# A hybrid decoder trunk in fp32: the last MLP's down projection, columns 1024 to 2047, by one level of Strassen

## The chip, the cores and the metric

The program runs on one core of a Trainium2 chip, one launch. The metric is the device time of that launch in microseconds, the median of several runs.

## The reference, cut to what matters

Two pre-norm residual layers over 256 tokens with 2048 features, float32. Each layer has a mixer (attention and retention heads in the first; state-space groups and a gated convolution in the second), a cross attention into 256 memory tokens, and an MLP with a hidden width of 8192:

```
def sq_relu_mlp(xn, w1, w2):
    return jnp.square(jax.nn.relu(xn @ w1)) @ w2

for layer in range(2):
    h = h + mixer(rmsnorm(h, norm_mix[layer]))
    h = h + cross_attention(rmsnorm(h, norm_xattn[layer]), memn, ...)
    h = h + sq_relu_mlp(rmsnorm(h, norm_mlp[layer]), mlp_w1[layer], mlp_w2[layer])
return rmsnorm(h, norm_final)
```

w1 is 2048x8192 and w2 is 8192x2048. The change is in the product with w2 of the second (last) MLP.

## The kernel before, in words

**Precision.** Every matmul operand is a sum of a high part (fp32r, one pass of TensorE) and a low part (what rounding left). A product is three matmuls: high by high, high by low weights, low activations by high weights (lines 636 to 638). For each weight half ACT copies the raw fp32 weights into the high part `whi` (line 1267), and DVE subtracts it from the raw ones into `wlo` (line 1838). That pair of steps is called a split here.

**Slabs, halves and the ring.** Weights come in slabs of 1 MB (`raw`, four buffers; the DMAs are issued by SP, lines 408 and 423, when DVE has split what was there). A slab is two halves of 256 rows by 512 columns. `whi` and `wlo` have four places each (RING = 4), used in order: half n goes into place n mod 4. ACT may write place n when PE has used half n-4 (semaphore `half_used`); DVE waits for ACT (`hi_ready`), PE for DVE (`lo_ready`). A unit is eight halves.

**A chunk of the MLP.** The hidden width is cut into 8 chunks of 1024. A chunk is four units: two head units, each making 512 hidden values with the tokens as the moving operand (per half 8 wide matmuls of 512 columns, line 1073, and 8 narrow ones of 256, line 1081; two halves are taken together, first both wide groups, then both narrow ones, and the other way round in the last two halves); then two pair units of the down projection, for output columns 0 to 1023 and 1024 to 2047 (per half 12 matmuls of 512 columns). The first chunk's first unit has another form ("wide").

**PSUM.** `acc` has four banks, two for a block, and blocks alternate between the two pairs. A unit of either kind fills two blocks. PE waits on `acc_free` before it opens one. For a head unit's banks that release comes from DVE's reduction into `hid` (line 2223), for a pair unit's from DVE's adds into `h` (line 1886, two operations of 128x512, one for each 128 tokens). `tp` and `at`, two banks each, are used by transposes and attention, not by the MLP's later chunks.

**The order of the work.** Each engine runs a list written out by hand. On ACT and DVE a unit is a loop over i = 0..7: split half i, then what the slot i holds. On DVE: in the first head unit of a chunk, slots 1 and 2 hold the adds into `h` of the previous pair unit (columns 1024 to 2047); in the second head unit and the first pair unit, slots 0, 1, 2 hold the four reductions of the unit before (0; 1; 2 and 3), slots 3 and 5 the low part of the squared hidden values (line 2231); in the second pair unit slots 1 and 2 hold the adds of columns 0 to 1023. ACT does relu and square of the hidden values in slots 2 and 4 (lines 1624 to 1627), with the high part into `yt`. Chunks 1 to 6 of the last MLP run in a hardware loop, one chunk per trip. The scale of the norm is applied at the adds (`rstd[:, 14]`, the square of the reciprocal root, since the squared relu is homogeneous).

At the end, POOL multiplies `h` by the final gain (vector loaded by a DMA), and ACT and DVE finish the last norm.

Of the kernel before, what the change touches and what calls it, by code (L numbers as in the profile page):

```python
# [23 lines left out]
F32 = mybir.dt.float32  # L24
# [4 lines left out]
ALU = mybir.AluOpType  # L29
AX = mybir.AxisListType  # L30

P = 128
# [71 lines left out]


def trunk(nc, x, mem, norm_final, ab_w_in, ab_b_forget,
          ab_w_out, cd_w_in, s5_d, s5_w_glu, cd_w_out, xa_wq, xa_wkv, xa_wo, mlp_w1, mlp_w2,
          rope, decay_in, tri, causal, eye, x_t, mem_t, gains, s5_rates, s5_bc, fb_d, out):
    ctx = ExitStack()
    with ctx:  # L110
# [19 lines left out]

        rstd = sb("rstd", [P, 15, TOK])
        ssq = sb("ssq", [P, TOK, BLOCKS])
# [182 lines left out]
        hg_ready, fin_act = sem("hg_ready"), sem("fin_act")  # L315
        fin_ready, out_done = sem("fin_ready"), sem("out_done")

        par_of = {n: i for i, n in enumerate((
# [28 lines left out]

        OB = 4 + 14 + 4 + 2 + 4 + 8 * CHUNKS - 1


# [49 lines left out]
        def _(sp):  # L400
# [8 lines left out]

            def load(kind, w, cols, order=(0, 1, 2, 3), row0=0, first=False, hook=None):  # L410

                for i in range(RING):
                    if kind == "query":
# [35 lines left out]
                    if hook:  # L449
                        hook(i)  # L450
                p.bump("half", 8)
                p.bump("unit")
# [128 lines left out]
            load("mixed", xa_wo[1], [n * NB for n in range(4)])  # L581
            mlp(1)

# [7 lines left out]
        def _(pe):  # L591
# [28 lines left out]
            def unit(kind, src, tok, after=None, order=(0, 1, 2, 3), kbase=0):  # L620

                hi, lo = src
                for i, (blk, kt0, opens, closes) in enumerate(plan(kind, order, kbase)):
                    par = (p.n["block"] + blk) % 2
                    if opens and p.n["block"] + blk >= 2:

                        pe.wait_ge(acc_free[par], p.at("block", blk, by=2))
                    pe.wait_ge(lo_ready, p.at("half", i + 1))
                    for kk in range(2):
                        if kt0 + kk in tok:  # L630
                            wait_tp_read(pe, tok.pop(kt0 + kk))
                        for t in range(TOK):
                            a = acc[:, 2 * par + t, :]
                            xh, xl = (s[:, kt0 + kk, t * P:(t + 1) * P] for s in (hi, lo))
                            w = i % RING
# [10 lines left out]
            def final_pair(tok):  # L646
# [4 lines left out]
                def half(i, t):  # L651
                    blk, kt0, opens, closes = steps[i]
                    par = (p.n["block"] + blk) % 2
                    for kk in range(2):
                        a = acc[:, 2 * par + t, :]
                        xh, xl = (s[:, kt0 + kk, t * P:(t + 1) * P] for s in (hi, lo))
                        w = i % RING
                        pe.matmul(a, xh, whi[:, w, kk], start=opens and kk == 0, stop=False)
# [451 lines left out]

            def mlp(final, params=None, tables=None):
                apart = TAB_CHUNKS if tables else ()
                trips = CHUNKS - 2 - len(apart)

                def step(first, last, beside=None, t0=0):
# [23 lines left out]
                    if last and final:  # L1139
                        final_pair(y_tok)  # L1140
                    else:
                        unit("pair", yt, y_tok, last_after if last else u_after(3))
                step(True, False, params)
                with pe.Fori(0, trips) as r:
# [6 lines left out]

            attention_and_out(0, lambda i: h_block(3, 1) if i == 0 else None)
            mlp(False, None, s5_tables)


# [84 lines left out]
            attention_and_out(1, lambda i: h_block(2 + i, 2 - i) if i < 2 else None)  # L1240
            mlp(True)


        @block.scalar
        def _(act):
# [11 lines left out]
            def split(i, kind):  # L1257
# [7 lines left out]
                if p.n["half"] + i >= RING or p.reg is not None:  # L1265
                    act.wait_ge(half_used, p.at("half", i - RING + 1))
                act.activation(split_weights(whi, kind, i), half_weights(raw, kind, i), ACT.Copy)\  # L1267
                   .then_inc(hi_ready, 1)
# [346 lines left out]

            def hidden_squares(j, kt0, wide):

# [10 lines left out]

            def mlp(layer, row, next_row, final, params=None, tables=None):
                apart = TAB_CHUNKS if tables else ()  # L1630
                wide_at[0] = p.n["at"]
# [3 lines left out]
                def step(first, last, beside=None, t0=0):  # L1635
                    def slot_of(u):
                        def slot(i):
# [10 lines left out]
                            if last and u == 3:  # L1648
                                if i == 2:
                                    h_squares(0, 2)  # L1650
                                if i == 4:
                                    h_squares(1, 1)
                                if not final and i in (3, 5):
                                    hi_parts(xt, 0 if i == 3 else 4, next_row)
# [19 lines left out]
            attention_and_out(0, xq_first, MLP)  # L1674
            mlp(0, 3, MIX + 16, False, s5_params, s5_tables)

# [122 lines left out]
            attention_and_out(1, xq1_first, MLP + 16)  # L1799
            mlp(1, 6, None, True)  # L1800
            act.wait_ge(ssq_ready, p.n["ssq"])
# [19 lines left out]
        def _(dve):  # L1821
# [11 lines left out]
            def unit(kind="full", slot=None, ahead=None):  # L1833
                for i in range(HALVES):
                    if ahead:
                        ahead(i)
                    dve.wait_ge(hi_ready, p.at("half", i + 1))
                    dve.tensor_tensor(split_weights(wlo, kind, i), half_weights(raw, kind, i),  # L1838
                                      split_weights(whi, kind, i).bitcast(F32), ALU.subtract).then_inc(lo_ready, 1)
                    if slot:  # L1840
# [362 lines left out]

            def mlp(layer, m, next_row, final, params=None, tables=None):

# [28 lines left out]

                apart = TAB_CHUNKS if tables else ()
                trips = CHUNKS - 2 - len(apart)

                def step(first, last, beside=None, t0=0):
                    def slot_of(u):
                        def slot(i):  # L2240
# [27 lines left out]
                            if u == 3:  # L2268
                                if i == 1:
                                    add_block(0, 2, -2, 13 + layer)  # L2270
                                if i == 2:
                                    add_block(1, 1, 0, 13 + layer)
                                if last and not final and i in (4, 6):
                                    lo_parts(xt, 0 if i == 4 else 4, next_row)
# [23 lines left out]
            attention_and_out(0, xq_first, 2, MLP)  # L2298
            mlp(0, 3, MIX + 16, False, s5_params, re_tables)
            p.bump("at", 1 + 16 + 2)  # L2300
# [201 lines left out]
            attention_and_out(1, xq1_first, 5, MLP + 16)  # L2502
            mlp(1, 6, None, True)

# [20 lines left out]
        def _(pool):  # L2525
# [262 lines left out]

            wait_block(OB + 9 + 4 + 2 + 4 + 2 + 4)
            pool.dma_start(gfin, norm_final.rearrange("(a n) -> a n", a=1).to_broadcast([P, D]))\  # L2790
# [3 lines left out]
            for b in range(2):  # L2794
                wait_block(OB + 9 + 4 + 2 + 4 + 2 + 4 + 8 * CHUNKS - 1 - 4 + b)
                c = slice(b * NB, (b + 1) * NB)
# [57 lines left out]
```

## Time and profile before

| | |
|---|---|
| median of 3 runs | 2395.32 us (2393.95 to 2397.63) |
| profiled execution | span 2393.6 us; no other time of it is given |
| PE busy | 2381.2 us, 99% of the span |
| DVE busy | 1486.0 us, 62% |
| ACT busy | 1178.8 us, 49% |
| granted clock of TensorE | 1.00 through the last MLP |
| one chunk of the last MLP | 88.0 us |

Busy time is the time in which the engine has an instruction running. PE is matmuls, PEld weight loads beside them. A matmul's end is modelled and overlaps the next one's start: the start-to-start time is what counts, for DVE and ACT too where operations follow each other directly. The clock column gives the share of full speed that TensorE was granted.

### The profile page before, as it was taken

Reading aid. Unit: us, or ns where it says so; the run is one execution under the profiler, and the core shown is the slowest. Engines: PE = TensorE matmul, PEld = TensorE weight load, DVE = VectorE, ACT = ScalarE, POOL = GpSimd, SP = SyncE. Lnnn points to the kernel's source line nnn. Section 1 sums busy time; section 2 is a strip of 40 time slices with the busy share of each in tenths; the row PEclk is TensorE's granted clock in tenths of the full one; section 3 lists DMA queues with packets and bytes.
Section 4 is the critical chain, followed back from the end, with each engine's and each line's share of the span. In section 5 each row is a group of like instructions: output and inputs, shape, how many; then the busy total and the mean of one; then the engine's idle time right before and its main releaser. Section 6 shows DMA issues by size and latency. Waiting matters only on the chain.

```text
span 2393.6 us, 31780 instructions
## 1 busy us (share of the span) xinstructions
PE 2381.2 (99%) x12434; PEld 2013.9 (84%) x12434; DVE 1486.0 (62%) x1872; ACT 1178.8 (49%) x1573; POOL 343.1 (14%) x469
## 2 busy tenths in 40 slices
PE   9999999999999999999999999999999999999998
PEld 7888888888888888888888888889888888888887
DVE  5546455556655657878856657566655556555556
ACT  7544545546544444444445445556634444444444
POOL 0033120003173003545510100000000000000000
PEclk9999999999999999999999999999999999999999
DMA  9755565564666667787885869865666666556663
GB/s 356 269 162 189 183 209 169 177 189 148 193 191 190 189 192 229 238 255 227 260 272 188 231 211 264 264 194 159 195 192 193 193 191 193 189 181 197 190 191 123
DMA packets 341363, 492.23 MB, mean 206 GB/s; under 512 B 18792, under 2 KB 184528, under 8 KB 340992
## 3 DMA queue, kind: packets, MB, share of 16 engines
q1 hardware_dynamic: 316096, 464.03, 61.4%
q0 software_dynamic: 3888, 14.02, 1.9%
q10 hardware_dynamic: 21264, 12.59, 1.7%
q8 instruction: 78, 1.28, 0.2%
q14 instruction: 37, 0.30, 0.0%
HBM read 475.72 MB, written 19.08 MB: 207 GB/s over the span
## 4 chain that ended last, share of the span: by engine, by line
PE 96%; DVE 2%; ACT 1%; DMA 0%; issue 0%; SPq 0%; ACTq 0%; DVEq 0%
PE acc L636 19%; PE acc L638 19%; PE acc L637 19%; PE acc L1073 19%; PE acc L1081 10%; PE at L723 2%; PE tp L699 1%; PE at L1043 1%; PE acc L1043 1%; DVE wlo L1838 1%; PE tp L723 1%; PE acc L945 1%; PE acc L943 1%; PE acc L944 1%; ACT whi L1267 1%; DMA raw<-in_xa_wkv 0%
## 5 line engine op out<-in xcount | busy, mean ns | idle before, releaser
L1838 DVE TENSOR_TENSOR wlo<-raw,whi 128x1024 fp32r<-128x1024 f32 x824 | 1044.1, 1274 | 800.7 <-ACT whi L1267 797.3
L1267 ACT ACTIVATE whi<-raw 128x1024 fp32r<-128x1024 f32 x824 | 864.4, 1059 | 1002.2 <-PE acc L638 574.7
L636 PE MATMUL acc<-whi,yt_hi 128*128 128x512 f32 x1408 | 552.5, 392 | 1.5 <-DVE h L1886 1.5
L638 PE MATMUL acc<-whi,yt_lo 128*128 128x512 f32 x1408 | 548.2, 389 | 0.0
L637 PE MATMUL acc<-wlo,yt_hi 128*128 128x512 f32 x1408 | 548.0, 389 | 0.0
L1073 PE MATMUL acc<-x,whi 128*128 128x512 f32 x1984 | 474.7, 391 | 0.0
L1073 PEld LDWEIGHTS acc<-x,whi 128*128 128x128 f32 x1984 | 365.1, 188 | 71.9 <-issue 0.8
L636 PEld LDWEIGHTS acc<-whi,yt_hi 128*128 128x128 f32 x1408 | 264.3, 188 | 57.9 <-issue 2.0
L638 PEld LDWEIGHTS acc<-whi,yt_lo 128*128 128x128 f32 x1408 | 264.3, 188 | 55.4
L637 PEld LDWEIGHTS acc<-wlo,yt_hi 128*128 128x128 f32 x1408 | 264.4, 188 | 53.8
L636 PE MATMUL acc<-whi,x 128*128 128x512 f32 x672 | 265.9, 396 | 0.0
L1081 PEld LDWEIGHTS acc<-x,wlo 128*128 128x128 f32 x1984 | 253.7, 191 | 9.9 <-issue 0.8
L638 PE MATMUL acc<-whi,x 128*128 128x512 f32 x672 | 261.9, 390 | 0.0
L637 PE MATMUL acc<-wlo,x 128*128 128x512 f32 x672 | 261.7, 389 | 0.0
L1081 PE MATMUL acc<-x,wlo 128*128 128x256 f32 x1984 | 257.3, 283 | 0.0
L2535 POOL TENSOR_TENSOR arena<-arena 128x32 f32<-128x32 f32 (+5 forms) x275 | 193.5, 703 | 361.4 <-DMA arena<-fp_d 179.0
L636 PEld LDWEIGHTS acc<-whi,x 128*128 128x128 f32 x672 | 126.2, 188 | 26.7 <-issue 1.2
L638 PEld LDWEIGHTS acc<-whi,x 128*128 128x128 f32 x672 | 126.1, 188 | 26.7
L637 PEld LDWEIGHTS acc<-wlo,x 128*128 128x128 f32 x672 | 126.3, 188 | 25.1
L2797 POOL TENSOR_TENSOR arena<-h,arena 128x1024 f32<-128x1024 f32 x2 | 5.7, 2862 | 659.4 <-DVE h L1886 659.4
L1886 DVE SCALAR_TENSOR_TENSOR h<-acc,rstd,h 128x512 f32<-128x512 f32 x124 | 87.1, 744 | 8.7 <-PE acc L638 8.7
L2223 DVE TENSOR_REDUCE arena<-acc 128x256 f32<-128x512 f32 x124 | 82.2, 683 | 0.0
(232 smaller groups left out, 1511.9 us busy)
## 6 DMA issues: line engine op xcount, KB each, us to landing
raw<-in_mlp_w SPq DMA_DIRECT2D x256, 1024.0 KB, 5.6
raw<-in_ab_w_in SPq DMA_DIRECT2D x56, 1024.0 KB, 5.1
raw<-in_cd_w_in SPq DMA_DIRECT2D x32, 1024.0 KB, 5.7
raw<-in_ab_w_out SPq DMA_DIRECT2D x16, 1024.0 KB, 5.1
raw<-in_cd_w_out SPq DMA_DIRECT2D x16, 1024.0 KB, 6.9
raw<-in_xa_wkv SPq DMA_DIRECT2D x14, 1024.0 KB, 11.7
raw<-in_xa_wq SPq DMA_DIRECT2D x16, 512.0 KB, 4.6
raw<-in_xa_wo SPq DMA_DIRECT2D x8, 512.0 KB, 4.6
```

The source lines that it names most:

```text
L636: pe.matmul(a, xh, whi[:, w, kk], start=opens and kk == 0, stop=False)
L637: pe.matmul(a, xh, wlo[:, w, kk], start=False, stop=False)
L638: last = pe.matmul(a, xl, whi[:, w, kk], start=False, stop=closes and kk == 1)
L723: return pe.matmul(o, lhsT, rhs, start=start, stop=stop)
L1043: last = pe.matmul(o.rearrange("p (a n) -> p a n", a=2), whi[:, w, kk, c], x2[:, :, 2 * i + kk, :], start=i == 0 and kk == 0, stop=closes ...
L1073: last = pe.matmul(head(i).rearrange("p (a n) -> p a n", a=2), split_weights(whi, "heads", i)[:, kk, :], x2[:, :, k0 + kk, :], start=i < 4 ...
L1081: last = pe.matmul(head(i)[:, 0:L], split_weights(wlo, "heads", i)[:, kk, :], x2[:, 0, 8 * (i // 4) + kk, :], start=False, stop=i >= 4 and ...
L1267: act.activation(split_weights(whi, kind, i), half_weights(raw, kind, i), ACT.Copy)\
L1838: dve.tensor_tensor(split_weights(wlo, kind, i), half_weights(raw, kind, i), split_weights(whi, kind, i).bitcast(F32), ALU.subtract).then_ ...
L1886: last = dve.scalar_tensor_tensor(out=hb, in0=acc[:, 2 * par_ + t, :], scalar=rstd[:, row, t:t + 1], in1=hb, op0=ALU.mult, op1=ALU.add)
L2223: ins = dve.tensor_reduce(hid[:, hh, :], bank.rearrange("p (a n) -> p n a", a=2), AX.X, ALU.add)
L2535: link(pool.tensor_tensor(o, a, b, op))
```

## The change

In chunks 0 to 6 the second pair unit is gone. In its place stand seven block products: activations [A11 A12; A21 A22] (128 tokens by 512 hidden values each) times weights [B11 B12; B21 B22] (512x512 each, kept raw in four arena buffers of 1 MB, `sraw`, loaded by their own DMAs). Products P1 and P2 take plain blocks; the others take combinations: DVE forms four combinations of hidden values in place (`a11`, `a21`, `a12`, `a22` over `hid` and a new `hid2`) and adds weight blocks in place in `sraw` (`raw_sum`, eight operations of 128x1024 per chunk). Each product is two halves (a and b in the text) of 6 matmuls, accumulated in the banks `at` and `tp`, where P6, P7 and P3 join the running sums of P1 and P5; eight adds into `h` (`evict`) take them out, two of them for P7, with plus or minus the scale.

The 14 product halves share the ring with the 24 plain ones. They are put behind halves of the next chunk's head units (P6, then P5, P4, P7, P3) and of the chunk's own pair unit (P1, P2), after the table `S_BEHIND`. ACT, DVE and PE all take this order; on DVE and ACT's list the order within slot i is: split of half i; on DVE then splits of the product halves behind it, then the slot's other work; on ACT the slot's work, then the product halves. Chunk 7 keeps two plain pair units. The hardware loop has 3 trips of two chunks. The adds of columns 0 to 1023 of chunks 0 to 6 now stand in slots 1 and 2 of the next head unit. The final gain is loaded when the last chunk's first pair unit begins.

```diff
+S_BEHIND = {(0, 5): (("p6", 0),), (0, 7): (("p6", 1),),
+            (1, 1): (("p5", 0), ("p5", 1)), (1, 3): (("p4", 0), ("p4", 1)),
+            (1, 5): (("p7", 0), ("p7", 1)), (1, 7): (("p3", 0), ("p3", 1)),
+            (2, 1): (("p1", 0),), (2, 3): (("p1", 1),), (2, 5): (("p2", 0),), (2, 7): (("p2", 1),)}
+S_SLOT = {"p1": 0, "p5": 0, "p7": 1, "p2": 2, "p4": 2, "p6": 3, "p3": 3}
+S_KT = {"p1": (0, 0), "p2": (4, 0), "p4": (4, 1), "p6": (8, 0), "p7": (8, 1), "p3": (12, 0), "p5": (12, 1)}
...
+        hid2 = view(1024, 1024, "p (b n) -> p b n", b=4)
+        sraw = [view(2048 * (n + 1), 2048, "p (k n) -> p k n", k=4) for n in range(4)]
...
 # SP: loads of a pair unit, hook(i) after slab i
+                        if i == 0:
+                            ...
+                                sp.wait_ge(lo_ready, p.at("half", PLACE_OF["p5", 1] + 1))
+                            s_load(0, row0, 0)
+                        if i == 1:
+                            if again is not None:
+                                sp.wait_ge(t_sum, p.at("s", 1) * 8)
+                                s_load(3, again + NB, 1)
+                                sp.wait_ge(lo_ready, p.at("half", PLACE_OF["p4", 1] + 1))
+                            s_load(2, row0 + NB, 0)
+                        if i == 2:
+                            ...
+                            s_load(1, row0, 1)
+                        if i == 3:
+                            ...
+                            s_load(3, row0 + NB, 1)
...
 # PE
+                for kk in range(2):
+                    xh, xl = (v[:, kt + 2 * j + kk, t * P:(t + 1) * P] for v in yt)
+                    pe.matmul(o, xh, whi[:, w, kk], start=opens and j == 0 and kk == 0, stop=False,
+                              skip_group_check=joins)
+                    pe.matmul(o, xh, wlo[:, w, kk], start=False, stop=False, skip_group_check=joins)
+                    last = pe.matmul(o, xl, whi[:, w, kk], start=False, stop=j == 1 and kk == 1,
+                                     skip_group_check=joins)
+                last.then_inc(half_used, 1)
...
 # DVE
+            def own_slots(u, i, first, final):
+                if u == 0:
+                    if i == 0:
+                        marked(formed["s2"])
+                        dve.scalar_tensor_tensor(out=a12, in0=a12, scalar=-1.0, in1=a11, op0=ALU.mult,
+                                                 op1=ALU.subtract).then_inc(form_sum, 1)
+                        raw_sum(0, 1, 1, split="p1")
+                        raw_sum(1, 3, 0, (s_in[3], p.at("s") * 32 + 16), after=1)
+                    if i in (1, 2):
+                        add_block(i - 1, 3 - i, used[2, 3 + 2 * i] - p.n["half"], 14)
+                    if i == 2:
+                        raw_sum(3, 0, 0, after=3)
+                    if i == 3:
+                        form_lo(0)
+                        raw_sum(1, 3, 1, after=2)
+                    if i == 4:
+                        raw_sum(3, 0, 1, after=5)
+                    if i == 5:
+                        evict(1, "p2", tp[:, 0, :], ((0, 2),))
+                if u == 1:
+                    if i == 0:
+                        dve.wait_ge(form_ready, p.at("s") * 2 + 1)
+                    if i < 3:
+                        head_sum(1, i)
+                    if i == 0:
+                        form_lo(1)
+                    if i == 1:
+                        raw_sum(2, 3, 0, after=4, split="p2")
+                    if i == 2:
+                        head_sum(1, 3)
+                        raw_sum(2, 3, 1, after=6, split="p2")
+                        evict(2, "p6", at[:, 0, :], ((0, 3),))
+                    if i in (3, 5):
+                        head_lo(1, i // 2 - 1)
+                    if i == 4:
+                        evict(3, "p5", at[:, 1, :], ((1, 3),))
+                    if i == 6:
+                        evict(4, "p4", tp[:, 1, :], ((1, 2),))
+                if u == 2:
+                    if i == 0 and not first:
+                        evict(-2, "p7", at[:, 0, :], ((1, 2), (1, 3)))
+                        dve.wait_ge(form_ready, p.at("s") * 2)
+                    if i < 3:
+                        head_sum(2, i)
+                    if i == 2:
+                        head_sum(2, 3)
+                        if not first:
+                            evict(-1, "p3", at[:, 1, :], ((0, 3),))
+                    if i in (3, 5):
+                        head_lo(2, i // 2 - 1)
+                    if final:
+                        return
+                    if i == 6:
+                        dve.wait_ge(hid_ready, p.at("hid"))
+                        formed["s1"] = mark(dve.tensor_tensor(a22, a22, a21, ALU.subtract))
+                    if i == 7:
+                        marked(formed["s1"])
+                        formed["s3"] = mark(dve.tensor_tensor(a21, a11, a21, ALU.subtract))
+                        evict(None if first else 0, "p1", at[:, 0, :], ((0, 2),))
+                        marked(formed["s3"])
+                        formed["s2"] = mark(dve.scalar_tensor_tensor(out=a11, in0=a11, scalar=-1.0, in1=a22,
+                                                                     op0=ALU.mult, op1=ALU.subtract))
+                        raw_sum(0, 1, 0, (s_in[1], p.at("s", 1) * 16), split="p1")
+
+            def blend(u, first=False, final=False):
+                kind = "pair" if u == 2 else "heads"
+                for i in range(HALVES):
+                    dve.wait_ge(hi_ready, p.at("half", 1))
+                    ...
+                    if not final:
+                        for name, j in behind(u, i):
+                            s_lo(name, j)
+                    own_slots(u, i, first, final)
```

## Rows read from the trace of the kernel before

**Rows 1.** Page, part 1: busy time, share of the span and instructions of each engine.

```profile
PE 2381.2 (99%) x12434; PEld 2013.9 (84%) x12434; DVE 1486.0 (62%) x1872; ACT 1178.8 (49%) x1573; POOL 343.1 (14%) x469
```

**Rows 2.** Windows of one chunk: length, busy time of each engine, clock, DMA.

```profile
core 0: us, PE busy (x) PEld busy (x) DVE busy (x) ACT busy (x) POOL busy (x), PEclk, DMA share, GB/s
2032.99:2121.00 88.01, 88.01 (x450) 75.40 (x449) 51.24 (x52) 39.78 (x44) 0.00 (x0) 1.00 0.60 190
```

**Rows 3.** PE's two longest waits: released by, us in total, times, longest us.

```profile
PE acc L636 <- DVE h L1886: 1.5, 1, 1.5
PE at L723 <- DVE arena L1822: 1.2, 1, 1.2
```

**Rows 4.** Timeline, chunk boundary: start, length, engine, line, operation, idle time before.

```profile
2203.62 1.06 ACT L1267 ACTIVATE whi<-raw 128x1024 fp32r<-128x1024 f32 x1 [1.66 <-PE acc L638]
...
2204.71 1.23 DVE L1838 TENSOR_TENSOR wlo<-raw,whi 128x1024 fp32r<-128x1024 f32 x1 [1.49 <-ACT whi L1267]
...
2205.85 1.40 DVE L1886 SCALAR_TENSOR_TENSOR h<-acc,rstd,h 128x512 f32<-128x512 f32 x2
...
2206.14 0.39 PE L636 MATMUL acc<-whi,yt_hi 128*128 128x512 f32 x1
...
2206.34 1.06 ACT L1267 ACTIVATE whi<-raw 128x1024 fp32r<-128x1024 f32 x1 [1.66 <-PE acc L638]
...
2209.06 1.41 DVE L1886 SCALAR_TENSOR_TENSOR h<-acc,rstd,h 128x512 f32<-128x512 f32 x2 [0.40 <-PE acc L638]
2210.39 1.22 DVE L1838 TENSOR_TENSOR wlo<-raw,whi 128x1024 fp32r<-128x1024 f32 x1
```

**Rows 5.** Timeline of PE: last pair matmuls of a chunk, then head halves.

```profile
2199.79 0.39 PE L638 MATMUL acc<-whi,yt_lo 128*128 128x512 f32 x1
...
2208.63 0.39 PE L638 MATMUL acc<-whi,yt_lo 128*128 128x512 f32 x1
2208.86 3.79 PE L1073 MATMUL acc<-x,whi 128*128 128x512 f32 x16
2212.49 2.08 PE L1081 MATMUL acc<-x,wlo 128*128 128x256 f32 x16
2214.40 3.82 PE L1073 MATMUL acc<-x,whi 128*128 128x512 f32 x16
```

**Rows 6.** Timeline of DVE: reductions between splits.

```profile
2227.00 0.68 DVE L2223 TENSOR_REDUCE arena<-acc 128x256 f32<-128x512 f32 x1
2227.61 1.22 DVE L1838 TENSOR_TENSOR wlo<-raw,whi 128x1024 fp32r<-128x1024 f32 x1
...
2234.38 0.68 DVE L2231 TENSOR_TENSOR yt_lo<-arena,yt_hi 128x512 fp32r<-128x512 f32 x1
```

**Rows 7.** Timeline of an earlier chunk boundary, POOL busy.

```profile
1009.68 1.65 DVE L1838 TENSOR_TENSOR wlo<-raw,whi 128x1024 fp32r<-128x1024 f32 x1
...
1011.25 1.40 DVE L1886 SCALAR_TENSOR_TENSOR h<-acc,rstd,h 128x512 f32<-128x512 f32 x2
...
1012.71 0.50 PE L636 MATMUL acc<-whi,yt_hi 128*128 128x512 f32 x1 [1.49 <-DVE h L1886]
...
1013.05 0.40 PE L637 MATMUL acc<-wlo,yt_hi 128*128 128x512 f32 x1
```

**Rows 8.** DMA issues by target: count, KB, us to landing.

```profile
raw<-in_mlp_w SPq DMA_DIRECT2D x256, 1024.0 KB, 5.6
...
arena<-in_norm_final POOLq DMA_DIRECT2D x1, 1024.0 KB, 5.1
```

**Rows 9.** Windows, columns as in rows 2: one early, two at the end.

```profile
20.00:30.00 10.00, 10.00 (x44) 8.27 (x45) 9.15 (x12) 6.85 (x10) 0.00 (x0) 1.00 1.05 386
...
2386.00:2390.00 4.00, 0.00 (x0) 0.00 (x0) 2.24 (x7) 1.94 (x4) 0.00 (x0) 0.87 0.35 135
2390.00:2393.60 3.60, 0.00 (x0) 0.00 (x0) 0.00 (x0) 0.00 (x0) 0.00 (x0) 0.50 0.73 291
```

**Rows 10.** Timeline of PE: its last matmul.

```profile
2384.66 0.39 PE L660 MATMUL acc<-whi,yt_lo 128*128 128x512 f32 x1
```

More of the change, by code:

```diff
@@ L1138, in last_after @@
                             h_block(1, 1)
[L1139 to L1143, printed above, removed]
+                    unit("pair", yt, y_tok, last_after if last else u_after(3))
+                step(True, False)
                 with pe.Fori(0, trips) as r:
@@ new lines, in _ @@
+            p.n["s"] = 0
+            pair_blend(y_tok, True)
+            with pe.Fori(0, BLEND_TRIPS) as r:
+                p.enter(r, BLEND_RATES)
+                for _ in range(2):
+                    hidden_blend(0)
+                    hidden_blend(1)
+                    p.bump("s")
+                    hid_tokens()
+                    pair_blend(y_tok)
+                p.leave(BLEND_TRIPS)
+            hidden_blend(0)
+            hidden_blend(1)
+            hid_tokens()
+            unit("pair", yt, y_tok)
@@ new lines, in blend @@
+            def blend(u, slot):
+                kind = "pair" if u == 2 else "heads"
+                for i in range(HALVES):
+                    if i % 2 == 0:
+                        loads = p.bump(f"slab{i // 2}")
+                        act.wait_ge(raw_landed[i // 2], loads * 16)
+                    act.wait_ge(half_used, p.at("half", 1 - RING))
+                    act.activation(split_weights(whi, kind, p.n["half"]), half_weights(raw, kind, i), ACT.Copy)\
+                       .then_inc(hi_ready, 1)
+                    p.bump("half")
+                    slot(i)
+                    for name, j in behind(u, i):
+                        s_split(name, j)
+                p.bump("unit")
+                p.bump("block", 2)
@@ L1801, in _ @@
+            blend(0, form_slots)
+            blend(1, lambda i: own_squares(i, 0))
+            unit("pair", lambda i: own_squares(i, 4))
+            unit("pair", last_pair)
             act.wait_ge(ssq_ready, p.n["ssq"])
@@ new lines, in blend @@
+            def blend(u, first=False, final=False):
+                kind = "pair" if u == 2 else "heads"
+                for i in range(HALVES):
+                    dve.wait_ge(hi_ready, p.at("half", 1))
+                    n = p.n["half"]
+                    dve.tensor_tensor(split_weights(wlo, kind, n), half_weights(raw, kind, i),
+                                      split_weights(whi, kind, n).bitcast(F32), ALU.subtract).then_inc(lo_ready, 1)
+                    p.bump("half")
+                    used[u, i] = p.n["half"]
+                    if not final:
+                        for name, j in behind(u, i):
+                            s_lo(name, j)
+                    own_slots(u, i, first, final)
+                p.bump("unit")
+                p.bump("block", 2)
@@ new lines, in first_heads, with last_pair @@
+            def first_heads(i):
+                if i == 1:
+                    wide_sums()
+                if i in (3, 5):
+                    head_lo(1, i // 2 - 1)
+            def last_pair(i):
+                if i == 1:
+                    add_block(0, 2, -2, 14)
+                if i == 2:
+                    add_block(1, 1, 0, 14)
+            unit("wide", wide_slots)
+            unit("heads", first_heads)
+            used.update({(1, i): p.n["half"] - HALVES + i + 1 for i in range(HALVES)})
@@ L2505, in _ @@
+            blend(0)
+            blend(1)
+            blend(2, final=True)
+            unit("pair", last_pair)
             dve.wait_ge(cst["gf"], 16)
```

342 lines of the change are left out of this document (316 added, 26 removed).

## The prediction

> **What bounds the kernel now.** I read the busy table first, then the windows over the last MLP, then the waits of PE, then the timelines of PE, ACT and DVE around one boundary between two units. The busy table gives PE 2381.2 us of a span of 2393.6 [rows 1]. In the last MLP a chunk lasts 88.0 us; PE is busy for all of it, DVE for 51.2 and ACT for 39.8 [rows 2]. PE's longest wait for another engine in the whole program is 1.5 us, the next 1.2 [rows 3]. So what counts is the number of columns that PE streams and whether anything makes it wait; idle time of DVE and ACT costs nothing as long as PE's next operand and its next bank are there.
>
> They are there only by a small margin, which decides this case. Around 2208.86 (plain pairs end, the first head unit of the next chunk begins) the first PSUM bank pair is given back by the two DVE adds that begin at 2205.85 and last 1.40, so at 2207.25; PE asks for it at 2208.86, 1.6 us later [rows 4].
>
> **Prices.** All from the traced chunk.
> - A 512-column matmul starts every 0.2267 us (40 of them from 2199.79 to 2208.86) [rows 4, 5]. A half of a pair unit (12) is 2.72 us; a half of a block product (6) is 1.36. A pair of head halves is 16 wide (3.65) and 16 narrow ones (1.91), 5.56 [rows 5].
> - Hand-over. PE ends a half at 2206.14 (the next half's first matmul starts); ACT's copy for the half four places later starts at 2206.34: +0.20. ACT's copy starts at 2203.62, the DVE subtraction that needs it at 2204.71: +1.09 [rows 4].
> - DVE, start to start in a queue: subtraction 1.14 (2204.71 to 2205.85), PSUM add into h 0.665 (1.33 for two, 2209.06 to 2210.39) [rows 4], reduction 0.605 (2227.00 to 2227.61), low part of 128x512 0.60 taken like it; the last one of a chain costs its whole length, 0.745 and 0.68 [rows 6].
> - PE once held by a DVE add is in the trace too, the same kind of wait: the adds end at 1012.65, PE starts at 1012.71, and its second matmul comes 0.34 later where 0.23 is usual: 0.17 on top of every chain [rows 7].
>
> **What it removes.** Eight block products of 12 matmuls become seven in 7 chunks: 7 x 12 = 84 matmuls, 84 x 0.2267 = 19.0 us. Every one lay on PE's path. PE's own work of a chunk falls from 88.0 to 85.3 us.
>
> **What it adds beside PE.** Per chunk: 6 more splits (ACT copy and DVE subtraction), 8 sums of weight halves on DVE (128x1024, both sources in SBUF), 4 combinations of the hidden activations (128x512), 2 copies on ACT and 2 subtractions on DVE of 128x1024 for their parts, 8 adds into h for 4. DVE by its start-to-start prices: before 32 x 1.14 + 8 x 0.665 + 8 x 0.605 + 4 x 0.60 = 49.0; added 14 x 1.14 + 4 x 0.665 + 2 x 0.60 + 2 x 0.665 + 2 x 1.14 = 23.4; 72.5 of at least 85.3 us. ACT: 39.8 + 8 x 1.06 = 48.3. So neither becomes the bound by its total. One more 1 MB transfer per chunk (17 for 16): 17 MB in some 90 us is about 200 GB/s, where a stretch near the start moved 386 [rows 9], and each is issued 12 us or more before its reader; no cost. A weight sum stands in no row: the nearest is the subtraction of the same size (1.14). Ends: 0.60 (half as large an operation) and 1.65 (the subtraction beside a busy POOL [rows 7]). I take 1.14, as nothing runs on POOL here.
>
> **What it moves, and the waits that this makes.** The weight ring keeps its four places, but now 38 halves pass through it, and DVE does all of this in one fixed order. PE's bank for a unit is freed by a DVE operation that stands *behind* the second split of that unit (slot 1). Write H1, H2, D for the head units and the pair unit, a and b for a product's halves. The order at the three boundaries: D4 D5 P2a D6 D7 P2b | H1.0 H1.1; H1.6 H1.7 P6b | H2.0 H2.1 P5a P5b; H2.6 H2.7 P3a P3b | D0 D1 P1a. A split waits until PE has finished four places before.
>
> *Boundary B, start of H2.* Its first bank pair is freed by the reduction that now stands behind the splits of H2.1, P5a and P5b. P5b goes into the place of P6b, the very last work that PE has. So PE ends P6b, then 0.20 + 1.09 + 1.14 + 0.68 = 3.11, + 0.17: **3.28 us** with PE idle, however idle DVE is. 7 times: 23.0.
>
> *Boundary C, start of D.* The reduction stands behind the splits of D0, D1 and P1a and behind the two adds of P7. H2.6 is released 4.55 before PE runs out (a wide group of 1.83 and P3's 2.72), D0's subtraction starts at -4.55 + 0.20 + 1.09 = -3.26; then 1.14 + 2 x 0.665 + 0.605 + 1.14 + 1.14 + 0.68 = 6.04: +2.78, + 0.17: **2.95 us**, 6 times. In the first chunk (no P3 in front, no add of P7) H2.6 is released at -1.83, P1a's split starts at -0.53, ends the chain at 1.29: 1.46. In the last (no P1a behind D1) the chain ends at 1.63: 1.80. Together 17.7 + 3.3 = 21.0.
>
> *Boundary A, start of H1.* Count from PE's end of D4. PE then has D5, P2a, D6, D7, P2b: 10.88 us. DVE splits D7 early, but P2b's place is freed by D5 (2.72), so its subtraction starts at 2.72 + 0.20 + 1.09 = 4.01. Queued in front of the add that frees the bank: that subtraction 1.14, a combination 0.60, the add of P1 0.665, a combination 0.665, a weight sum 1.14, split H1.0 1.14, a combination 0.665, two weight sums 2.28, split H1.1 1.14, the first add 0.665, the second to its end 0.745: 10.85. That is 14.86, + 0.17 = 15.03, against 10.88: **4.15 us**, 7 times: 29.1.
>
> *A small one, D'.* The second bank pair of H2 comes with the reductions behind H2.2, whose place H2.0 frees 4.6 us into the unit: 4.6 + 0.20 + 1.09 + 1.14 + 0.605 + 0.68 = 8.32 + 0.17 against 5.56 + 2.72 = 8.28: 0.2, 7 times: 1.4.
>
> Following DVE on through the chunk, it has caught up with PE by H1.6 and again by D3, so the lateness of one boundary isn't handed to the next. Steady chunk: 85.3 + 4.15 + 3.28 + 0.2 + 2.95 = 95.9 us for 88.0.
>
> **Sum.** Stalls 29.1 + 23.0 + 21.0 + 1.4 = 74.5; removed 19.0; net +55.5. Rest: the tail's final gain vector is loaded later, but still some 20 us before its reader (the first split of D in the last chunk against the first of the last two adds of a pair unit), and it lands in 5.1 [rows 8]; ends of both kernels are the same work. The profiled span is 2393.6, of whose execution no other time is shown; the median of the three runs is 2395.3, so 1.7 lie around it. 2393.6 + 55.5 + 1.7 = 2450.8; I say **2451 us**.
>
> **The clock, and the rule that speaks against the change.** TensorE's granted clock is 1.00 (2.4 GHz) all through the last MLP. After PE's last matmul (it ends at 2385.05 [rows 10]) the stretch 2386 to 2390 shows 0.87 and the next 0.50 [rows 9]: the fall lies at about 2389, some 3.9 us after it. Stall A leaves the array idle for 4.15 - 0.16 = 4.0 us. The trace has no gap of length between 1.5 us [rows 3] and this one, so whether A lowers the clock is open.
>
> The Trainium skill (TensorE: Matmul & The Clock Gate, "Why this matters for your kernels") tells that an idle gap between bursts of matmuls puts the clock back to its half rate, and warns of just such gaps as this change brings. By that rule the time would be the clock rival's below rather than my sum; the trace agrees that the clock falls after an idle stretch, with the 0.87 above.
>
> **The rivals.**
> - *The clock falls at A.* At 1.2 GHz the same columns take twice as long. If it stays low over the first head pair (5.56 us of work), that is +5.6 each, 7 x 5.6 = 39: 2490; at half of the boundaries 2470. For: A is as long as the idle time before the fall. Against: B and C are shorter. 13%.
> - *PE stays the bound, the gain is real.* The mechanism would be that PE never runs out at A, B and C: the place would be the release in slot 1, it would have to come before PE has emptied the ring. Price -19.0: 2376. It decides where DVE's queue in front of the release is under PE's remaining work (10.88 at A, 0 at B). For: DVE's total fits (72.5 of 85). Against: B is only a chain of hand-overs, and cannot be shorter than 3 us. 4%.
> - *Only A goes.* DVE's sums run at 0.60 and it is ahead by D7: 2451 - 29 = 2422. For: no row has a sum. Against: twelve operations are needed. 8%.
> - *Transfers late.* Three are issued together behind H2.3, and the block for P3 has 12.6 us until its reader; the first one lands after 5.6 and the others some 2.7 each later [rows 8], leaving 1 to 4 us. If each were 4 us late, 6 x 4 = 24: 2475. 5%.
>
> The forecast itself has 70%. Its own range: three sums in A by their ends, 3 x (-0.54 to +0.51) x 7 = 11 either way: 2440 to 2462. The range for 8 in 10 takes in the case without A below and most of the clock and transfer cases above: 2422 to 2484. What a measurement can tell from no change is 0.2%, about 5 us; all cases but one end above that: slower 0.94, faster 0.04, within 0.02.
>
> **What would show it.** Three gaps of PE in each steady chunk: in front of the first wide matmul of H1 and of H2 and of the first matmul of D, each ended by DVE (an add into h at A, a reduction at B and C), of 4, 3 and 3 us, 20 in all; PE's busy time smaller by some 19 us; DVE some 180 us busier (26 a chunk by the lengths of its operations); chunk period near 96. Wrong would be: gaps only at A (DVE's load is all), gaps that end with ACT or a DMA, matmuls 0.43 apart behind a gap (clock), or a period of 85.

## The result, and the profile after

The changed kernel takes 2485.6 us (median of 4 runs, 2483.8 to 2486.3), the one before 2395.5: ratio 1.0375, interval 1.0361 to 1.039. The forecast was 2451 with a range to 2484: the direction was right, the size was not, and the time lies just above the range.

Busy times of the changed kernel, whose span is 2483.2 us (before: [rows 1]):

```profile
PE 2398.7 (97%) x12350; PEld 2016.2 (81%) x12350; DVE 1642.1 (66%) x2041; ACT 1236.0 (50%) x1629; POOL 345.3 (14%) x469
```

PE is busy 17.5 us *longer* although 84 matmuls went (2381.2 to 2398.7), and its idle time grew from 12.4 to 84.5. Who ends that idle time is in PE's waits (released by, us in total, times, longest):

```profile
PE acc L1393 <- DVE h L2189: 29.6, 7, 5.5
PE acc L1393 <- DVE arena L2830: 21.5, 7, 3.1
PE acc L1431 <- DVE arena L2830: 18.6, 7, 2.9
```

Twenty-two gaps: the 20 long ones that the prediction counts, and the two short ones before D that its sum has and its count leaves out. Seven stand before H1 (ended by an add into h, L2189), seven before H2 and seven before D (by the reduction L2830; D's first gap is half as long), and one before D of the last chunk, 1.6 us, which stands under another line (L747). Before, the longest wait was 1.5 us [rows 3]. One steady chunk, as in [rows 2]:

```profile
core 0: us, PE busy (x) PEld busy (x) DVE busy (x) ACT busy (x) POOL busy (x), PEclk, DMA share, GB/s
...
1962.58:2064.15 101.57, 91.86 (x437) 76.76 (x437) 73.61 (x77) 47.92 (x52) 0.00 (x0) 0.94 0.54 176
```

It lasts 101.6 us for 88.0, with PE busy 91.9 of them where the count of matmuls gives 85.3, at a granted clock of 0.94.

The gap before H1, first as PE's last matmul before it and the first behind it, then as DVE's list in the same time (start, length, line; in square brackets the idle time before, and what ended it):

```profile
1855.37 0.39 PE L1376 MATMUL tp<-whi,yt_lo 128*128 128x512 f32 x1
1859.54 6.40 PE L1393 MATMUL acc<-x,whi 128*128 128x512 f32 x16 [3.78 <-DVE h L2189]
```

```profile
1848.73 1.23 DVE L2846 TENSOR_TENSOR wlo<-arena,whi 128x1024 fp32r<-128x1024 f32 x1 [1.49 <-ACT whi L2040]
1849.87 0.68 DVE L2950 TENSOR_TENSOR arena<-arena 128x512 f32<-128x512 f32 x1
1850.47 0.74 DVE L2858 SCALAR_TENSOR_TENSOR h<-at,rstd,h 128x512 f32<-128x512 f32 x1
1851.13 0.68 DVE L2953 SCALAR_TENSOR_TENSOR arena<-arena 128x512 f32<-128x512 f32 x1
1851.73 1.22 DVE L2871 TENSOR_TENSOR arena<-arena 128x1024 f32<-128x1024 f32 x1
1852.87 1.21 DVE L2962 TENSOR_TENSOR wlo<-raw,whi 128x1024 fp32r<-128x1024 f32 x1
1854.00 0.68 DVE L2897 SCALAR_TENSOR_TENSOR arena<-arena 128x512 f32<-128x512 f32 x1
1854.60 2.35 DVE L2871 TENSOR_TENSOR arena<-arena 128x1024 f32<-128x1024 f32 x2
1856.88 1.21 DVE L2962 TENSOR_TENSOR wlo<-raw,whi 128x1024 fp32r<-128x1024 f32 x1
1858.01 1.40 DVE L2189 SCALAR_TENSOR_TENSOR h<-acc,rstd,h 128x512 f32<-128x512 f32 x2
```

This is the queue that the prediction adds up for boundary A, operation by operation: P2b's split (1848.73), a combination, the add of P1, a combination, a weight sum, split H1.0, a combination, two sums, split H1.1 and the two adds that free the bank. It lasts from 1848.73 to 1859.41, 10.7 us (forecast 10.85). PE ran out at 1855.60.

The gap before H2, all engines, is the bare chain of hand-overs: PE ends P6b (last start 1785.02), ACT copies P5b into that place at 1785.44, DVE's split of it is the second of the two that begin at 1785.18, the reduction starts at 1787.68, PE at 1788.49.

```profile
1785.02 0.39 PE L1376 MATMUL at<-whi,yt_lo 128*128 128x512 f32 x1
1785.18 2.58 DVE L2846 TENSOR_TENSOR wlo<-arena,whi 128x1024 fp32r<-128x1024 f32 x2 [0.59 <-ACT whi L2040]
1785.44 1.06 ACT L2040 ACTIVATE whi<-arena 128x1024 fp32r<-128x1024 f32 x1 [0.30 <-PE at L1376]
1787.68 0.68 DVE L2830 TENSOR_REDUCE arena<-acc 128x256 f32<-128x512 f32 x1
...
1788.49 0.49 PE L1393 MATMUL acc<-x,whi 128*128 128x512 f32 x1 [3.08 <-DVE arena L2830]
```

What the prediction's sum leaves out is the clock. The windows (third column from the end: granted clock) show it in and behind four gaps. The first four lines are one gap before H1: inside it, around the fall, over the first wide matmuls behind it, and around the rise. Then come a gap before H2 behind which it did not fall, one before D behind which it did, and the first gap before H1 with the 16 wide matmuls behind it:

```profile
1856.00:1859.00 3.00, 0.00 (x0) 0.00 (x0) 3.00 (x4) 2.33 (x3) 0.00 (x0) 0.84 0.00 0
1858.00:1858.50 0.50, 0.00 (x0) 0.00 (x0) 0.50 (x2) 0.33 (x1) 0.00 (x0) 0.56 0.00 0
1859.54:1865.90 6.36, 6.36 (x18) 5.03 (x19) 6.36 (x7) 0.00 (x0) 0.00 (x0) 0.58 0.63 176
1864.50:1865.00 0.50, 0.50 (x3) 0.40 (x2) 0.50 (x1) 0.00 (x0) 0.00 (x0) 0.61 0.00 0
...
1890.38:1894.10 3.72, 3.72 (x16) 3.09 (x17) 1.00 (x1) 0.00 (x0) 0.00 (x0) 1.00 0.95 317
1926.97:1934.00 7.03, 7.03 (x18) 5.54 (x19) 3.15 (x5) 2.62 (x4) 0.00 (x0) 0.56 0.42 126
...
1754.75:1758.54 3.79, 0.01 (x1) 0.01 (x1) 3.79 (x6) 2.58 (x3) 0.00 (x0) 1.00 0.06 14
1758.54:1764.06 5.52, 5.52 (x18) 4.40 (x19) 5.52 (x6) 0.00 (x0) 0.00 (x0) 0.69 0.60 182
```

In the gap before 1859.54 it falls to half while PE stands, at about 1858.1, some 2.3 us after PE's last matmul. It stays there for about 5 us of work, until about 1864.6: 16 wide matmuls take 6.40 us at 1859.54 for the 3.8 of [rows 5]. In the gap before 1758.54, of the same length, it still reads 1.00 and falls only when PE is at work again; there the 16 take 5.52.

### The profile page after: what moved, and what is told of

The parts are those of the page before. It is cut to its first block, busy times and chain, and to the rows that moved or that the text cites. A ratio compares the mean times of both kernels' runs of the same rounds, so it can differ in the third digit from the quotient of the medians.

```text
span 2483.2 us, 32175 instructions
## 1 busy us (share of the span) xinstructions
PE 2398.7 (97%) x12350; PEld 2016.2 (81%) x12350; DVE 1642.1 (66%) x2041; ACT 1236.0 (50%) x1629; POOL 345.3 (14%) x469
## 4 chain that ended last, share of the span: by engine, by line
PE 89%; DVE 5%; issue 3%; ACT 2%; DMA 0%; DVEq 0%; SPq 0%; ACTq 0%
PE acc L747 14%; PE acc L749 14%; PE acc L748 14%; PE acc L1184 10%; PE acc L1393 9%; PE acc L1192 5%; PE acc L1402 4%; PE acc L1431 2%; PE acc L1432 2%; PE acc L1433 2%; PE at L834 2%; PE tp L810 1%; PE at L1373 1%; PE at L1375 1%; PE at L1376 1%
## 5 line engine op out<-in xcount | busy, mean ns | idle before, releaser
L2141 DVE TENSOR_TENSOR wlo<-raw,whi 128x1024 fp32r<-128x1024 f32 x592 | 761.7, 1293 | 541.4 <-ACT whi L1494 538.3
L1494 ACT ACTIVATE whi<-raw 128x1024 fp32r<-128x1024 f32 x600 | 630.7, 1059 | 663.0 <-PE acc L749 402.4
L747 PE MATMUL acc<-whi,yt_hi 128*128 128x512 f32 x960 | 378.4, 394 | 3.3 <-DVE h L2189 1.8
L749 PE MATMUL acc<-whi,yt_lo 128*128 128x512 f32 x960 | 374.1, 390 | 0.0
L748 PE MATMUL acc<-wlo,yt_hi 128*128 128x512 f32 x960 | 373.8, 389 | 0.0
L2051 ACT ACTIVATE whi<-raw 128x1024 fp32r<-128x1024 f32 x168 | 176.4, 1058 | 282.1 <-PE acc L1402 173.2
L2962 DVE TENSOR_TENSOR wlo<-raw,whi 128x1024 fp32r<-128x1024 f32 x176 | 214.8, 1220 | 145.4 <-ACT whi L2051 136.7
L1393 PE MATMUL acc<-x,whi 128*128 128x512 f32 x896 | 233.9, 417 | 51.1 <-DVE h L2189 29.6
L747 PE MATMUL acc<-whi,x 128*128 128x512 f32 x672 | 265.9, 396 | 0.0
L1184 PE MATMUL acc<-x,whi 128*128 128x512 f32 x1088 | 262.5, 391 | 0.0
L747 PEld LDWEIGHTS acc<-whi,yt_hi 128*128 128x128 f32 x960 | 180.3, 188 | 42.5 <-DVE h L2189 2.2
L749 PEld LDWEIGHTS acc<-whi,yt_lo 128*128 128x128 f32 x960 | 180.2, 188 | 38.0
L748 PEld LDWEIGHTS acc<-wlo,yt_hi 128*128 128x128 f32 x960 | 180.4, 188 | 36.4
L2846 DVE TENSOR_TENSOR wlo<-arena,whi 128x1024 fp32r<-128x1024 f32 x98 | 117.9, 1221 | 53.2 <-ACT whi L2040 52.3
L747 PEld LDWEIGHTS acc<-whi,x 128*128 128x128 f32 x672 | 126.2, 188 | 26.4 <-issue 1.2
```

The source lines that it names most:

```text
L1184: last = pe.matmul(head(i).rearrange("p (a n) -> p a n", a=2), split_weights(whi, "heads", i)[:, kk, :], x2[:, :, k0 + kk, :], start=i < 4 ...
L1393: last = pe.matmul(head(i).rearrange("p (a n) -> p a n", a=2), split_weights(whi, "heads", p.n["half"] + i % 2)[:, kk, :], x2[:, :, 8 * (i ...
L1494: act.activation(split_weights(whi, kind, p.n["half"] + i), half_weights(raw, kind, i), ACT.Copy)\
L2051: act.activation(split_weights(whi, kind, p.n["half"]), half_weights(raw, kind, i), ACT.Copy)\
L2141: dve.tensor_tensor(split_weights(wlo, kind, n), half_weights(raw, kind, i), split_weights(whi, kind, n).bitcast(F32), ALU.subtract).then_ ...
L2846: dve.tensor_tensor(wlo[:, w], sraw[S_SLOT[name]][:, 2 * j:2 * j + 2, :], whi[:, w].bitcast(F32), ALU.subtract).then_inc(lo_ready, 1)
```

## The experiments

All are edits of the changed kernel, timed against the kernel before on the same chip (2394.4 to 2395.2 there). The expectations set theories against each other. By the order theory a gap is made by what stands in DVE's list before the operation that frees the bank; the ring theory is its part about the four places. By the load theory DVE simply has too much to do. By the clock theory the matmuls behind a gap are slow because the granted clock fell.

**Reductions ahead of the first split of H2 and D.**

```diff
                 for i in range(HALVES):
+                    if i == 0 and u:
+                        if u == 1:
+                            dve.wait_ge(form_ready, p.at("s") * 2 + 1)
+                        elif not first:
+                            dve.wait_ge(form_ready, p.at("s") * 2)
+                        head_sum(u, 0)
+                        head_sum(u, 1)
                     dve.wait_ge(hi_ready, p.at("half", 1))
```

(and out of slots 0 and 1)

> The first two reductions of H2 and of D stand ahead of those units' first split; nothing else changes. Order theory: PE's gaps in front of H2 (3.08 us each) and of D (2.83) go, those in front of H1 (3.79, and 5.2 to 5.5 at the jump of the hardware loop) stay. 7 x 3.2 + 6 x 3.0 + 1.6 = 42 us of gaps go, and the slow clock behind them, of 36.5 us in all about 15: 2485.6 - 57 = about 2428. Load theory (DVE has too much to do in total, 26 us more a chunk): the same operations are done, so the gaps come back elsewhere, above all at H1: 2475 or more.

Measured: 2424.3 us, ratio 1.0122 (1.0101 to 1.0142). PE's waits:

```profile
PE acc L1393 <- DVE h L2189: 30.0, 7, 5.6
```

The gaps before H2 and D are gone, the seven before H1 are the same (29.6 us in the changed kernel, 30.0 here). The same operations on DVE, 61 us less: these gaps came from the order and not from the load.

**The pair unit's adds earlier.**

```diff
-                    if i in (1, 2):
-                        add_block(i - 1, 3 - i, used[2, 3 + 2 * i] - p.n["half"], 14)
+                    if i == 1:
+                        add_block(1, 1, used[2, 7] - p.n["half"], 14)
...
                     if i == 7:
+                        add_block(0, 0, used[2, 5] - p.n["half"], 14)
                         marked(formed["s1"])
```

> The adds of the pair unit move: block 0 from slot 1 of H1 into D's slot 7 behind P2b's split, block 1 from slot 2 to slot 1 of H1. Order theory: the gap in front of H1 goes (29.6 us) with the slow clock behind it (about 21), the gaps at H2 and D stay at 3.08 and 2.83: about 2435. Load theory: about 2480, gaps at H2 or D grow.

Measured: 2448.2 us, ratio 1.0221 (1.0201 to 1.0242), 13 above what was expected. PE's waits:

```profile
PE acc L1393 <- DVE arena L2830: 21.5, 7, 3.1
PE acc L1431 <- DVE arena L2830: 18.6, 7, 2.9
...
PE acc L1393 <- DVE h L2189: 0.4, 2, 0.2
```

The gaps are as expected: H1's gone, the others unchanged to the tenth. The miss is the clock: it now falls behind every gap before H2 (the first wide group takes 5.5 us instead of 3.9 in seven of seven), where in the changed kernel it did so twice. PE's busy time is 27.7 us over the count of its matmuls, and 36.5 in the changed kernel, so only 9 went with seven gaps, not 21. What the clock costs isn't a sum over gaps, each with its own price. Why the gap before H2 is hit more often when the one before H1 is gone, no run shows.

**Both, and the weight sums of H1's slots 0 to 4 later.**

```diff
                     if i == 2:
-                        raw_sum(3, 0, 0, after=3)
+                        raw_sum(0, 1, 1, split="p1")
+                        raw_sum(1, 3, 0, (s_in[3], p.at("s") * 32 + 16), after=1)
                     if i == 3:
                         form_lo(0)
-                        raw_sum(1, 3, 1, after=2)
+                        raw_sum(3, 0, 0, after=3)
                     if i == 4:
-                        raw_sum(3, 0, 1, after=5)
+                        raw_sum(1, 3, 1, after=2)
                     if i == 5:
+                        raw_sum(3, 0, 1, after=5)
```

(the first two out of slot 0)

> Both edits, and the weight sums of H1's slots 0 to 4 two slots later (same order). Order theory: no gap over 0.3 us in the last MLP, clock 1.00, chunk period 85.3 to 86, time 2395.5 - 19.0 = 2376.5, up to 2385 if DVE (73 us of operations in 85) is late in places. Load theory: still 2450 or more. If it comes out faster than the kernel before, the block products themselves do pay.

Measured: 2379.4 us, ratio 0.9933 (0.9916 to 0.995). Two chunks' windows and PE's waits over the whole program:

```profile
1752.24:1837.84 85.60, 85.60 (x438) 73.07 (x436) 73.17 (x77) 47.89 (x52) 0.00 (x0) 1.00 0.64 209
1837.84:1923.46 85.62, 85.62 (x437) 72.89 (x436) 72.31 (x76) 47.90 (x52) 0.00 (x0) 1.00 0.65 209
```

```profile
PE at L834 <- DVE arena L2124: 1.2, 1, 1.2
PE acc L747 <- DVE h L2189: 0.9, 1, 0.9
PE tp L834 <- DVE yt_lo L2329: 0.6, 2, 0.3
PE acc L717 <- ACT yt_hi L1537: 0.3, 1, 0.3
PE acc L1184 <- DVE arena L2526: 0.2, 1, 0.2
```

No gap is left in the last MLP, the clock is 1.00, a chunk lasts 85.6 us. DVE is busy for 73 of them by the lengths of its operations: full, but never late where PE asks. This version takes 15.3 us less than the kernel before.

**Idle matmuls in the gaps.**

```diff
+            def fill_gap(n):
+                for _ in range(n):
+                    pe.matmul(tp[:, 1, :].rearrange("p (a n) -> p a n", a=2), x2[:, 0, 0, 0:P], x2[:, 0, 0:2, :],
+                              start=True, stop=True)
```

(17 before the wait of H1, 13 of H2, 11 of D; in front of those at D, PE also waits until the bank that they write is free)

> The changed kernel, and in each gap PE runs idle matmuls of 512 columns into a bank that nothing uses then: 17 before H1, 13 before H2, 11 before D, each a bit less than the gap. They add no work to the path. Clock theory (the 36.5 us by which PE's busy time is over the count of its matmuls come from the granted clock behind gaps): clock 1.00, gaps end when they did, time 2485.6 - 36.5 = about 2449. Rival (matmuls behind a gap are long because their operands come late): no change, 2485.

Measured: 2456.8 us, ratio 1.0257 (1.0237 to 1.0278). The granted clock over the whole execution is 0.999, for 0.985 in the changed kernel. The gap before H1 that cost 6.40 us above, now filled:

```profile
1851.25 4.01 PE L1383 MATMUL tp<-x 128*128 128x512 f32 x17
1855.19 3.92 PE L1399 MATMUL acc<-x,whi 128*128 128x512 f32 x16
```

28.8 us faster by doing 276 matmuls *more*. The first real matmul comes 3.94 us behind the last product, as in the changed kernel (1855.60 to 1859.54), so the wait is as it was and only the array isn't idle in it: about 30 us of the 90 lost are the clock's. The same from the changed kernel's own windows, of half a microsecond each: (1 - granted clock) x busy comes to 16.0 behind the seven gaps before H1, 11.0 behind the six long ones before D (the clock fell behind all of these), 3.4 behind those before H2 (two of seven), and nothing behind the two short ones. With the clock held, a chunk lasts 96.2 us (first matmuls of D at 1823.92 and 1920.11), for the 95.9 forecast. The rest of the 36.5 is no clock: every gap adds 0.16 of busy time in which the last matmul's end sticks out, and some 0.11 at the restart [rows 7], 22 x 0.27 = 5.9.

**Half-wide weight sums.**

```diff
-                o, a = (sraw[n][:, 2 * j:2 * j + 2, :] for n in (o, a))
+                o, a = (sraw[n][:, 2 * j:2 * j + 1, :] for n in (o, a))
```

This kernel leaves out half the rows of every weight combination, so it doesn't compute the product; it serves for its times alone.

> The changed kernel with the eight weight sums on half their rows only (the other half of each combination is left out, so part of the result is missing); order as it was. Three of them stand in front of the release before H1. Order theory: the gap before H1 gets shorter by 3 x (1.14 - 0.60) = 1.6 us, 3.8 to 2.2, those before H2 and D stay at 3.08 and 2.83 although DVE has 4.3 us less to do per chunk. Time 2485.6 - 11 = 2474, and down to 2455 if the clock then stays up at H1. Load theory: all three gaps shrink.

Measured: 2472.7 us, ratio 1.0323 (1.0302 to 1.0343). PE's timeline, a gap before H1 and one before H2:

```profile
2053.70 5.53 PE L1393 MATMUL acc<-x,whi 128*128 128x512 f32 x16 [2.19 <-DVE h L2189]
...
2083.72 4.62 PE L1393 MATMUL acc<-x,whi 128*128 128x512 f32 x13 [3.08 <-DVE arena L2830]
```

3.79 became 2.19, the 1.6 that was expected from the three sums in the queue; 3.08 and 2.83 stayed. With 30 us less to do on DVE in the whole program, no gap moved that has no sum in its queue. The clock still falls behind gaps of 2.2 us: of the five before H1 that have no loop jump in them, four have a first wide group of 5.5 us. Its part didn't shrink with the gaps: PE's busy time is 36.9 us over the count of its matmuls, for 36.5 in the changed kernel.

**P5b's split behind H2.3 instead of H2.1.**

```diff
-            (1, 1): (("p5", 0), ("p5", 1)), (1, 3): (("p4", 0), ("p4", 1)),
+            (1, 1): (("p5", 0),), (1, 3): (("p5", 1), ("p4", 0), ("p4", 1)),
```

> The changed kernel with one entry of the table moved: P5b goes from behind H2.1 to behind H2.3. The release before H2 then waits for P5a's split, which reuses the place of H1.7 and not of P6b, the last work before the gap. Ring theory: the gap before H2 gets shorter by P6b's length, 1.36 us: 3.08 to 1.7; the other two stay. 7 x 1.36 = 9.5, with the clock behind that gap up to 18: 2467 to 2476. Load theory: no gap changes, 2485.

Measured: 2470.1 us, ratio 1.0312 (1.0291 to 1.0332). The same two places:

```profile
2054.54 6.38 PE L1393 MATMUL acc<-x,whi 128*128 128x512 f32 x16 [3.78 <-DVE h L2189]
...
2084.01 3.93 PE L1393 MATMUL acc<-x,whi 128*128 128x512 f32 x16 [1.73 <-DVE arena L2830]
```

3.08 became 1.73: 1.35 less, for P6b's length of 1.36. Seven of seven gaps of 1.7 us have a first wide group of 3.9: behind these the clock didn't fall. The long gap before H1 keeps its 3.79.

**No hardware loop.** All six middle chunks written out on SP, PE, ACT and DVE (`for _ in range(CHUNKS - 2)` for the loop of three trips).

> The changed kernel without the hardware loop, all chunks written out. If the longer gaps before H1 (5.24 and 5.47 for 3.79, twice) are the loop's jump on DVE, every gap before H1 is 3.8 now, minus 3.1 us: about 2482. If they are something else (a late DMA), they stay.

Measured: 2473.9 us, ratio 1.0328 (1.0307 to 1.0348). The third gap before H1, 5.24 in the changed kernel:

```profile
1958.81 5.53 PE L1390 MATMUL acc<-x,whi 128*128 128x512 f32 x16 [3.71 <-DVE h L2180]
```

Every gap before H1 is 3.71 now, so the longer ones came with the loop's jump. In the changed kernel the jump stands in DVE's queue at this place, behind a weight sum:

```profile
1953.32 1.22 DVE L2871 TENSOR_TENSOR arena<-arena 128x1024 f32<-128x1024 f32 x1
1955.90 1.23 DVE L2962 TENSOR_TENSOR wlo<-raw,whi 128x1024 fp32r<-128x1024 f32 x1 [1.37 <-issue]
```

1953.32 + 1.14 would have been 1954.46; the split began at 1955.90. The time went down by 11.7, not by 3. The gaps without a jump are about 0.1 shorter each too, and the clock's part fell (the sum of (1 - granted clock) x busy over windows of 2 us from 1673 on is 30.0 in the changed kernel, 22.9 here).

**The order alone, the sums where they were.** The first two edits together.

> Reductions and adds moved as in the version with no gaps, the weight sums left where they were. Order theory: the release is all that counts; DVE's queue then ends the add of the second block 0.2 us before PE asks for it: 2377 to 2382. Rival: the two sums in H1's slot 0 make the second bank pair or the low parts of H1.1 late, by 1 us or more a chunk: 2385 to 2390.

Measured: 2379.6 us, ratio 0.9938 (0.9921 to 0.9955), no gap over 0.32 us. Where the sums stand makes no difference that the runs can tell once the releases are early (2379.4 with them later).

**The version without gaps once more, and without the loop.**

> The version without gaps once more, for an interval. By the count of matmuls, 19.0 us under the kernel before; the run before gave 15.3 under it. Expected ratio 0.993 to 0.994, about 2379; by a theory in which the block products cost what they save, 1.000.

> The version without gaps, the last MLP's chunks written out without the hardware loop. If what is left of the 19.0 us (some 3 us) comes from the loop's jumps, 2376 to 2377; if it lies in each chunk (the traced period is 85.6 where the count gives 85.3), 2379 as before.

Measured: 2378.6 us, ratio 0.9932 (0.9918 to 0.9945), and 2379.0 us, ratio 0.9932 (0.9919 to 0.9946). The jump costs nothing that the runs can tell where no release is held up behind it. The block products pay 15.8 us of the 19.0; some 2 us of the rest lie in the chunks (7 x 0.3), and where the last one went stays open.

## Why the prediction missed, step by step

**What is removed: right.** 84 matmuls, 19.0 us. With the gaps gone the chunk's period is 85.6 (forecast 85.3), and the kernel 15.8 faster.

**What is added on DVE hides, as total load: right.** DVE's busy time rose by 156 us (forecast some 180). The 180 adds up the lengths of the operations, but where two follow each other directly the profile's busy time counts the 0.08 us of their overlap only once; the prediction's own start-to-start prices, 23.4 a chunk, give 164. The load is hidden all the same: in the version without gaps all of it lies beside PE.

**Boundaries A, B, C: right in place, cause and size.** Idle, as the profile counts it, is the forecast less 0.27 (a modelled end of 0.16 and the restart's 0.11): A 3.88 forecast, 3.79 measured; B 3.01 and 3.08; C 2.68 and 2.83; D's first 1.2 and 1.57. Idle time in all rose by 72.1; with 5.9 for ends and restarts that is 78.0 of stalls for 74.5 forecast. The small one, D' (0.2 each), isn't there: PE's waits show none at that place. Not foreseen was the loop's jump in A's queue, 1.45 and 1.68 us more in two of seven: 3.1. Two of the chains were tested by a change of length: three half sums took 1.6 from A, P6b's place 1.35 from B. C had no such test of its own: it went when its release came early, and the trace has its two shorter forms, in the first chunk and the last (1.57 and 1.59, forecast 1.2 and 1.5).

**The sum: this step failed.** "Net +55.5" holds the granted clock at 1.00, and so puts the cost of slow matmuls behind the gaps at nothing; the prediction calls this open and sets it aside as a rival with 13%. Term by term in the profiled spans (2483.2 - 2393.6 = 89.6): -19.0 + 78.0 of stalls, and 30.6 left for the clock, which filling the gaps gave back but for 2. The clock belonged into the sum. That rival was right that the clock falls behind A (seven of seven), but its 5.6 us for each, 39 in all, was too much: it measured 2.3 each, 16.0. Its "against", that B and C are shorter, didn't hold: C took 11.0 us (six of six long ones) and B 3.4 (two of seven). In [rows 9] the fall was seen some 3.9 us behind the last matmul, and the text took that stretch for about what is needed; here 2.2 us of idle was enough in four of five, 1.7 in none of seven. The Trainium skill (TensorE: Matmul & The Clock Gate, "Why this matters for your kernels") warns of such gaps; the trace agrees (0.58 over 6.4 us behind a gap of 3.78), and parts from it on both sides: gaps shorter than the ones named there did it too (2.2 and 2.83 us), and five of the seven before H2 (3.0 to 3.1 us) did not. The rival's own 2470, for a fall at half of A's boundaries, would have been nearer than the sum, by luck: its price was too high and its places too few.

**The rivals.** "PE stays the bound" was wrong for this kernel and holds once its two groups of releases stand earlier. "Only A goes" did not happen; the sums are 1.14 start to start (1851.73 to 1852.87), as taken. "Transfers late": no gap ends with a DMA (the 2.7 us between landings, put down to [rows 8], stands in no row; it follows from 1 MB at the 386 of [rows 9]); the new loads land after 7.4 us (median of 35), two more than the old ones.

## What to carry to other kernels

When work is pushed into an engine's fixed list, look for the operation in it that frees a buffer, and count what now stands before it, not what the engine has to do in total: 22 us more per chunk (73.6 for 51.2) cost nothing once two reductions and two adds stood first. A ring place tells the earliest time of everything queued behind the item that waits for it; an item that reuses the place of PE's last work is a stall of a full hand-over (3.1 us here), whatever the load. And where PE gets gaps as long as these (2.2 us was enough in four of five), price the clock behind them as well, as a range, since no run here gives a price for one gap: it added four tenths to the stalls.

## What the runs showed of the hardware

The granted clock fell with every idle stretch of PE of 3.7 us and more and with every one of 2.72 to 2.86 (before D), with four of five of 2.1 to 2.2, and with none of 1.65 to 1.73 (seven), 1.56 to 1.59 or 1.5 [rows 3]. Behind a fall the first 16 wide matmuls took 5.5 to 6.8 us for 3.9. Which gaps it hits depends on more than their length: the gap of 3.0 to 3.1 before H2, longer than those before D, was followed by a slow group in two of seven cases in the changed kernel, in seven of seven once the gaps before H1 were gone, in three with the half sums and in one without the hardware loop. The fall can come inside the gap or when PE is at work again. The jump of the hardware loop lengthened a gap before H1 by 1.3 to 2.3 us, and cost nothing that the runs can tell where no gap stood behind it.
